# Late attention: scores behind three gate products, bias and maximum in one VectorE operation

## The reference, cut to what matters

```python
z = h @ w_in[l]
qa, ka, va, qs, ks_, vs, zg = jnp.split(z, splits, axis=-1)
...
o_na = neighbourhood_attention(qa, ka, va, na_rpb[l])
...
o_sw = sliding_window_gqa(qs, ks_, vs, t5_bias, sw_sink[l])
g = jax.nn.sigmoid((zg + b_gate[l]).astype(jnp.float32)).astype(x.dtype)
g = g.reshape(B, S, N_BRANCHES, D)
merged = g[:, :, 0] * (o_na @ w_branch_na[l]) + g[:, :, 1] * (o_sw @ w_branch_sw[l])
x = x + merged @ w_out[l]
```

```python
m = jnp.maximum(s.max(axis=-1, keepdims=True), sink_b)
e = jnp.exp(s - m)
p = e / (e.sum(axis=-1, keepdims=True) + jnp.exp(sink_b - m))
```

## Time and profile before

| | us |
|---|---|
| median of 3 runs | 2549.5 (2547.97 to 2552.3) |
| the profiled execution | 2545.43 |
| its span | 2544.1 |
| TensorE matmul (PE) busy | 2450.7 (96%) |
| VectorE (DVE) busy | 1279.6 (50%) |
| ScalarE (ACT) busy | 437.4 (17%) |
| GpSimd (POOL) busy | 179.6 (7%) |

### The profile page before, as it was taken

The page is one execution under the profiler, slowest core; times in us unless marked ns, Lnnn a source line. Parts: engine busy times, 40 slices in busy tenths (PEclk is TensorE's granted clock), DMA queues, the critical chain, the costliest instruction groups (busy, mean ns, idle before and its releaser), DMA issues.

```text
span 2544.1 us, 29717 instructions
## 1 busy us (share of the span) xinstructions
PE 2450.7 (96%) x12358; PEld 1568.2 (62%) x12358; DVE 1279.6 (50%) x2203; ACT 437.4 (17%) x1102; POOL 179.6 (7%) x126
## 2 busy tenths in 40 slices
PE   9999999889999999987889999999999999999999
PEld 5347443424578753332358857888866875888884
DVE  4994321212276521110117667665776775673774
ACT  2111110101123210000001102541101101560110
POOL 0011000000000000000000011430001003340000
PEclk9999999999999999999999999999999999999999
DMA  9854999999974499999999863425664974423671
GB/s 395 331 232 178 386 425 427 427 428 427 423 324 166 187 377 428 427 427 427 427 421 342 258 212 148 150 71 207 222 221 156 260 227 158 165 103 138 219 223 40
DMA packets 193618, 712.90 MB, mean 280 GB/s; under 512 B 117252, under 2 KB 121860, under 8 KB 128332
## 3 DMA queue, kind: packets, MB, share of 16 engines
q1 hardware_dynamic: 92304, 682.66, 67.3%
q10 hardware_dynamic: 101180, 28.35, 5.4%
HBM read 698.36 MB, written 12.60 MB: 279 GB/s over the span
## 4 chain that ended last, share of the span: by engine, by line
PE 77%; DMA 16%; DVE 5%; ACT 1%; issue 0%; POOL 0%; SPq 0%; another core or an unknown queue 0%; DVEq 0%; POOLq 0%
PE bank L865 75%; DMA ring<-in_stream 8%; DMA ring_high<-in_stream 4%; DMA ring_low<-in_stream 4%; PE bank L868 2%; DVE hidden L2887 1%; DVE ab_z L2712 1%; DMA hidden_turned<-normed 1%; DVE moe_results L2912 0%; DVE small L3456 0%; DVE hidden L3453 0%; DVE small L3459 0%; POOL ab_ln_sum L3583 0%; ACT hidden L2456 0%; DVE cd_y L2519 0%
## 5 line engine op out<-in xcount | busy, mean ns | idle before, releaser
L865 PE MATMUL bank<-ring,gates 128*128 128x256 f32 (+1 forms) x1760 | 433.7, 391 | 2.9 <-DVE ring L3223 1.9
L865 PE MATMUL bank<-ring,moe_chosen 128*64 128x512 f32 (+1 forms) x2352 | 400.5, 491 | 29.8 <-DMA ring<-in_stream 29.8
L865 PEld LDWEIGHTS bank<-ring,gates 128*128 128x128 f32 x1760 | 334.2, 190 | 69.9 <-issue 22.9
L865 PE MATMUL bank<-ring,normed 128*128 128x256 f32 x1448 | 339.7, 380 | 2.5 <-DMA ring<-in_stream 1.7
L865 PEld LDWEIGHTS bank<-ring,moe_chosen 128*64 128x64 f32 x2352 | 150.4, 137 | 249.6 <-issue 200.3
L865 PEld LDWEIGHTS bank<-ring,normed 128*128 128x128 f32 x1448 | 273.4, 190 | 42.0 <-issue 3.4
L865 PE MATMUL bank<-normed,ring 128*128 128x256 f32 (+2 forms) x1152 | 289.4, 406 | 2.4 <-DVE normed L2693 1.5
L865 PEld LDWEIGHTS bank<-normed,ring 128*128 128x128 f32 x1152 | 189.6, 191 | 98.5 <-issue 84.1
L865 PE MATMUL bank<-ring,ffn_hidden 128*128 128x512 f32 x352 | 170.7, 592 | 0.0
L2912 DVE COPY moe_results<-bank 32x512 f32<-32x512 f32 x36 | 24.8, 690 | 243.9 <-PE bank L865 243.6
L2903 DVE TENSOR_TENSOR moe_silu<-bank,moe_silu 128x512 f32<-128x512 f32 x32 | 22.1, 691 | 247.2 <-PE bank L865 247.2
(11 more groups left out here) (468 smaller groups left out, 2745.7 us busy)
## 6 DMA issues: line engine op xcount, KB each, us to landing
ring<-in_stream SPq DMA_DIRECT2D x318, 1024.0 KB, 7.3
ring<-in_stream SPq DMA_DIRECT2D x117, 2048.0 KB, 30.5
ring_low<-in_stream SPq DMA_DIRECT2D x7, 2048.0 KB, 43.1
ring_far<-in_stream SPq DMA_DIRECT2D x7, 2048.0 KB, 44.9
ring_high<-in_stream SPq DMA_DIRECT2D x6, 2048.0 KB, 44.6
hidden_turned<-normed ACTq DMA_DIRECT2D x44, 256.0 KB, 7.3
ffn_hidden<-hidden_turned ACTq DMA_DIRECT2D x44, 256.0 KB, 7.4
hidden<-in_stream SPq DMA_DIRECT2D x9, 1024.0 KB, 30.4
```

Source lines behind the costliest of these rows:

```text
L865: return nc.tensor.matmul(o, lhsT, rhs, start=start, stop=stop, skip_group_check=True)
```

## The change

On TensorE, pairs 1 to 7 run `turned(m - 1)`, `gates_first(m)`, `scores(m)`, `values(m - 1)`, `gates_rest(m)`. On VectorE, bias and maximum of a head are two operations of 128x256 (one for each half of the queries, t = 0 and 1), which write the negated biased scores and the negated maximum, with the negated sinks as the start value for sliding-window heads; these are made once a layer by one small operation. ScalarE negates again inside the exponential.

```diff
--- before.py
+++ after.py
@@ -619,6 +619,7 @@
     y.t1 = [y.KA[:, 2 * n:2 * n + 2, :] for n in range(2)]
     y.g8, y.stats = [M.small[:, 2 * l:2 * l + 2] for l in range(LAYERS)], M.small[:, 16:16 + 16 * 8]
     y.rinv_t, y.rinv_8 = M.small[:, 144:144 + TT], M.small[:, 146:146 + TT]
+    y.minus_sinks = M.small[:, 224:224 + SW_H]
     y.head_sums, y.head_roots = ([M.small[:, at + 16 * i:at + 16 * i + 16] for i in range(2)] for at in (160, 192))
     return M
 
@@ -1902,9 +1903,11 @@
         for m in range(pairs):
             if m:
                 turned(m - 1)
-            scores(m)
+            if m == 0:
+                scores(m)
             gates_first(m)
             if m:
+                scores(m)
                 values(m - 1)
             gates_rest(m)
             if m == 1:
@@ -2446,14 +2449,14 @@
             kind, blk = divmod(m, NA_H // 2)
             st = y.stats[:, 64 * (m % 2):64 * (m % 2) + 64]
             for i in range(2):
-                act.wait_ge(*V.at(("top", l, m, i)))
+                act.wait_ge(*V.at(("biased", l, m, i)))
                 if kind:
                     h = 2 * blk + i
                     nc.scalar.activation(st[:, 8 + 2 * i:10 + 2 * i], st[:, 2 * i:2 * i + 2], ACT.Exp,
                                          bias=M.sinks[:, l, h:h + 1]).then_inc(*done.up())
                 for t in range(TT):
                     n = 2 * i + t
-                    nc.scalar.activation(y.SC[i][:, t, :], y.SC[i][:, t, :], ACT.Exp, bias=st[:, n:n + 1],
+                    nc.scalar.activation(y.SC[i][:, t, :], y.SC[i][:, t, :], ACT.Exp, bias=st[:, n:n + 1], scale=-1.0,
                                          accum_out=st[:, 4 + n:5 + n]).then_inc(*done.up(("exp_2", l, m, i, t)))
 
         def turned(m):
@@ -3450,15 +3453,10 @@
                 h, top = 2 * blk + i, st[:, 2 * i:2 * i + 2]
                 if m:
                     dve.wait_ge(*TE.at(("turned_2", l, m - 1, i)))
-                v.tensor_tensor(y.SC[i], bank[i][:, :].rearrange("p (t k) -> p t k", t=TT), (y.SW_BIAS if kind else y.NA_BIAS)[:, h],
-                                ALU.add).then_inc(*done.up(("biased", l, m, i)))
-                dve.wait_ge(*done.now())
-                v.tensor_reduce(top, y.SC[i], AX.X, ALU.max, negate=True).then_inc(*done.up(None if kind else ("top", l, m, i)))
-                if kind:
-                    dve.wait_ge(*done.now())
-                    v.tensor_scalar(top, top, -1.0, M.sinks[:, l, h:h + 1], ALU.mult, ALU.max).then_inc(*done.up())
-                    dve.wait_ge(*done.now())
-                    v.tensor_scalar(top, top, -1.0, None, ALU.mult).then_inc(*done.up(("top", l, m, i)))
+                for t in range(TT):
+                    v.tensor_tensor_reduce(out=y.SC[i][:, t, :], in0=bank[i][:, T * t:T * t + T], in1=(y.SW_BIAS if kind else y.NA_BIAS)[:, h, t, :],
+                                           scale=-1.0, scalar=y.minus_sinks[:, h:h + 1] if kind else -3.0 * NEG, op0=ALU.add, op1=ALU.min,
+                                           accum_out=top[:, t:t + 1]).then_inc(*done.up(("biased", l, m, i) if t else None))
             for i in range(2):
                 total, extra = st[:, 4 + 2 * i:6 + 2 * i], st[:, 8 + 2 * i:10 + 2 * i]
                 dve.wait_ge(*A.at(("exp_2", l, m, i, TT - 1)))
@@ -3487,6 +3485,7 @@
             by_block = y.gates_of[c].rearrange("p (n t) -> p n t", t=T)
             v.tensor_tensor(by_block, by_block, wide(y.rinv, 2), ALU.mult).then_inc(*done.up(("gate", l, c)))
 
+        v.tensor_scalar(y.minus_sinks, M.sinks[:, l, :], -1.0, None, ALU.mult).then_inc(*done.up())
         dve.wait_ge(*done.now())
         dve.wait_ge(*S.chunk.at(("in_2", l, 8)))
         for m in range(NA_H):
```

## The result

| | before | after |
|---|---|---|
| median of the runs, us | 2548.61 (2546.07 to 2555.0) | 2554.95 (2551.84 to 2560.49) |
| ratio, 95% interval | | 1.0026 (1.0018 to 1.0034) |
| the profiled execution, us | 2545.43 | 2555.63 |
| transposes of pair 0 to those of pair 7, first layer | 67.90 | 71.49 |
| the same, second layer | 67.89 | 71.49 |

The change costs 6.3 us by the medians; the interval of the ratio is 4.6 to 8.7 us. The estimate lies just over the 0.2% that can be told here, and the lower end of its interval (0.18%) just under.

A forecast was written before the change was run, and what follows sets the result against it. TensorE's own order was taken as the bound. Stalls less saved shape changes lose 2.67 us a layer, 5.3 for two, so 2549.5 + 5.3 = 2554.8 us; range 2550.5 to 2559.5.

The forecast's parts named there:

- rival (a): TensorE, pairs 1 to 7: `gate_sums` arrives within the transposes' 0.89 us, so 4.4 us is won, 2545.1; chance 0.06.
- The stalls: TensorE at `gates_first`, behind the transposes: waits for VectorE's `gate_sums`, 0.79 us in pair 1, 0.45 in pair 2, 0.67 in pair 3.
- Nothing can go ahead: TensorE at `gates_first`: no gate product can run before `gate_sums`, since the gates write banks 4 and 5, which those sums read.
- The break-even: TensorE, per pair: the stall on `gate_sums` at which the new order neither wins nor loses, put at 0.21 us.
- Scores to values: TensorE's shape change from scores to values, absent from the earlier trace: taken as 0.13 us, bounds 0.12 and 0.19.
- The gap behind a stall: TensorE's shape change after a stall: shorter, 0.14 us instead of 0.18, so 0.04 off the loss.
- The fused operation: VectorE's bias and minimum in one operation of 128x256: 0.42 us, upper bound 0.68; ScalarE starts at 0.87.
- Rival (b): VectorE's fused operation runs at the scan's rate; pairs 3, 5, 6, 7 lose 0.44 us more each, 2558.3; chance 0.12.
- The readout: Reading out the fused operation's minimum on VectorE, perhaps an operation of its own: bounds 0 and 0.09 us, taken 0.04.
- The waits for L3471: Sliding-window pairs: second head's transposes wait for VectorE's probabilities; the 0.49 us pairs 6 and 7 lose would vanish.
- Rival (c): The stall is real but scores to values is free on TensorE: 1.8 us off, 2553.0; chance 0.08.

## Why the prediction was right, and which terms were mis-sized

The mechanism is the one forecast: a stall of `gates_first` on `gate_sums` in pairs 1 to 7 that costs more than the shape change saves. Taken out, the time is 2544.4; this is nearly the time that rival (a) gave for sums in time, 2545.1, though that rival had 4.4 us won where the trace shows 2 x 1.88 = 3.8. The median came out as forecast within 0.2 us. Some of that is chance, since the trace lost 3.59 a layer and my sum had 2.67, and the median of before fell by 0.9 as it was measured more often.

- **The stalls.** Reckoned from the end of the transposes' stream to the gates' load: 0.79, 0.45, 0.92, 0.67 and three times 0.77, 5.14 in all. Measured: 0.78, 0.52, 0.90, 0.73, 0.82, 0.83, 0.82, 5.40. I took 0.05 from VectorE's end to the load, from a transpose that waited for probabilities; here it is 1651.90 + 0.42 = 1652.32 to 1652.43, 0.11 (0.11 to 0.12 in all seven pairs). That term was some 0.06 too small in each pair. In pair 1 the sums came 0.08 sooner than in the rows of before, and pair 3 is late by 0.16 (1640.97 against 1640.50 + 0.31) where I had 0.25. This takes some of it back.
- **"Nothing can go ahead".** This was wrong. Of the three products of `gates_first` two write only the bank that the first sum, L3478 of before, has read by then; with the wait split they went ahead and the stall was gone. The change as it was made did not use this, so the forecast was not hurt by it.
- **The break-even.** The 0.21 that stands with rival (a) doesn't come out of its own terms: 0.24 saved and 0.04 off the next gap make 0.28 a pair. With the 0.19 measured, and nothing off, it is 0.19, and every stall was well over either.
- **Scores to values.** Taken 0.13, with 0.12 and 0.19 as bounds; it is 1646.23 - 1645.16 - 0.89 = 0.18. The row of the early filter was the wrong neighbour, and gates to values the right one. The saving is 0.19 a pair rather than 0.24: 0.35 a layer less. The prediction weighed the rule of the Trainium skill (TensorEngine Tiling (Array Packing), Key Properties) that a change of tiling mode drains the engine. By that rule this gap is not free, which the trace bears out; its price, which I had put at up to 0.19, is the measured 0.18.
- **The gap behind a stall.** I took 0.04 off, from transposes that had waited. Behind the stalled gates it is not shorter: 1645.16 - 1642.29 = 2.87, less 2.68, 0.19. Another 0.05 a pair, 0.35 a layer.
- These make up the difference pair by pair: 0.06 + 0.05 + 0.05 = 0.16, and pair 4 has a period of 1660.95 - 1650.81 = 10.14 where 9.59 + 0.39 = 9.98 was forecast. I had said 9.9 to 10.1.
- **The fused operation.** Taken 0.42, and ScalarE's start 0.87 behind the first; it is 0.42 and 0.48, and 0.81 and 0.93. Sliding-window heads take 0.06 more with a start value from memory, which I hadn't bounded apart. `gate_sums` of the sliding-window pairs is late by 0.09; I had 0.10. Rival (b), the rate of the scan, falls with this.
- **The readout** is an operation of its own, 0.08 within my bounds of 0 and 0.09, but it costs no time of its own, since the next fused operation starts at the same moment. The prediction cited the Trainium skill (VectorE: DVE Perf Modes, Two Vector instructions with no wait between them) for an accumulator output as a second instruction, and no run showed it then. The trace now agrees, with a row of its own of 0.08.
- **The waits for L3471** vanished as forecast: 0.51 a layer in the kernel with the fused operation alone, 0.49 in the sum.
- **Rival (c)**, scores to values for nothing, falls with the measured 0.18.

## What to carry to other kernels

Before a block of matmuls is moved, ask what it covers: these scores stood between TensorE and VectorE's sums, and moving them away cost 5.4 us a layer to save 1.3. When a stage saves a shape change and gains a wait, look whether another order saves the same change with the cover in place (values directly behind scores), or whether part of the waiting stage needs only an earlier event; both gave 2544.5 where the change gave 2555. A price for a shape change or a release is best taken from a row with the same shapes and the same kind of waiting instruction: all three of my misses came from a row with others.

## What the runs showed of the hardware that I had not expected

- VectorE held up by GpSimd: two multiplications of 128x256 from SBUF to SBUF took 2.52 us beside GpSimd's differences, and 0.62 when these were one element wide. An addition of 128x2 took 1.15 and then 0.16. The schedule before has such collisions as well (1.03 for 0.23), but only two pairs a layer wait behind them. Moving the scores brought them onto the steps that TensorE waits for, and with all that followed this cost some 19 us.
- A wait on TensorE can cost more than its length. Behind 3.92 us of it the granted clock was 0.53 and 16 instructions took 3.49 instead of 1.86; behind waits of 1.00 and 1.25 in a pair it was 0.62, between the levels, over the 24 gate instructions. Behind the stalls of the changed kernel, 0.5 to 0.9 us a pair, windows over both stretches show it full (1.00). Where between these it begins to fall, no run here tells.
- From the end of a VectorE operation to the load that it released were 0.05 us at a transpose and 0.11 to 0.12 at a gate product. Why they differ wasn't tried and stays open.
